# S5 layer: the late halves' entries moved ahead of all sixteen gate tiles, their copies split between ScalarE and VectorE

## The reference, cut to what matters

```python
pz = h @ w_in                     # D_MODEL -> 2 * E_WIDTH (E_WIDTH = 2048)
p, z = pz[..., :-E_WIDTH], pz[..., -E_WIDTH:]
# s5_mixer: u = p in 128 groups of 16 channels; for both directions:
def step(h, u_blk):
    bu = einsum('btgn,gpn->btgp', u_blk, bbar)      # enter the state space
    bu = bu.at[:, 0].add(abar[None] * h)
    _, hs = associative_scan(_linrec_combine, (a, bu), axis=1)   # recurrence
    y = einsum('btgp,gnp->btgn', hs, cmat).real      # leave it
...
g = gelu(y);  y = g * sigmoid(g @ w + bias)
x = layer_norm(alpha * x + gate * ((y * silu(z)) @ w_out), ...)
```

## Time and profile before

| | us |
|---|---|
| median of 3 runs | 2491.09 |
| lowest and highest | 2489.82, 2499.41 |
| profiled execution, its own time | 2490.22 |
| its span (first to last instruction) | 2488.4 |
| PE busy | 2179.3 (88%) |
| DVE busy | 1347.8 (54%) |
| ACT busy | 903.2 (36%) |

### The profile page before, as it was taken

The page is one execution under the profiler, slowest core; times in us unless marked ns, Lnnn a source line. Parts: engine busy times, 40 slices in busy tenths (PEclk is TensorE's granted clock), DMA queues, the critical chain, the costliest instruction groups (busy, mean ns, idle before and its releaser), DMA issues.

```text
span 2488.4 us, 33930 instructions
## 1 busy us (share of the span) xinstructions
PE 2179.3 (88%) x13589; PEld 1657.1 (67%) x13589; DVE 1347.8 (54%) x2633; ACT 903.2 (36%) x1779; POOL 445.0 (18%) x417
## 2 busy tenths in 40 slices
PE   6969897878989996899798976999999997878998
PEld 5847676647646695798453433678888864547998
DVE  4639676655578849454334456433333334455555
ACT  3325454542222273443222434222222212444443
POOL 0037969508911000000000000000000000000000
PEclk8989999989999998899899977899999998978999
DMA  8163545595687658865621312422323432224653
GB/s 276 57 204 108 168 122 143 163 275 180 213 268 219 193 197 320 232 170 181 192 68 51 102 35 87 131 93 86 96 81 93 115 102 85 85 81 140 196 162 118
DMA packets 434035, 366.34 MB, mean 147 GB/s; under 512 B 66238, under 2 KB 412622, under 8 KB 431702
## 3 DMA queue, kind: packets, MB, share of 16 engines
q1 hardware_dynamic: 392212, 320.87, 41.8%
q0 software_dynamic: 7424, 26.38, 2.9%
q10 hardware_dynamic: 34242, 16.92, 2.4%
HBM read 317.58 MB, written 54.92 MB: 150 GB/s over the span
## 4 chain that ended last, share of the span: by engine, by line
PE 68%; DVE 16%; ACT 6%; DMA 5%; POOL 2%; issue 2%; ACTq 1%; SPq 0%; DVEq 0%; POOLq 0%
PE ps L119 65%; DVE A L88 6%; PE ps L122 3%; ACT A L115 3%; POOL A L88 2%; DVE R L88 2%; DVE A L102 1%; DVE A L105 1%; DVE A L92 1%; DMA A<-btab 1%; DVE A L93 1%; DMA wbuf<-in_ada_w 1%; ACT A L116 1%; DVE A L96 1%; DMA xs<-X 1%
## 5 line engine op out<-in xcount | busy, mean ns | idle before, releaser
L119 PE MATMUL ps<-R,R 128*128 128x256 f32 (+1 forms) x3968 | 845.6, 335 | 35.5 <-ACT R L115 25.1
L119 PEld LDWEIGHTS ps<-R,R 128*128 128x128 f32 x3968 | 632.1, 193 | 109.6 <-ACT R L115 30.3
L119 PE MATMUL ps<-HR,R 128*128 128x512 f32 (+1 forms) x1984 | 556.8, 365 | 30.7 <-DVE R L88 20.5
L88 DVE TENSOR_TENSOR R<-wbuf,R 128x1024 fp32r<-128x1024 f32 (+2 forms) x304 | 349.5, 1158 | 350.6 <-ACT R L115 350.3
L119 PEld LDWEIGHTS ps<-HR,R 128*128 128x128 f32 x1984 | 358.1, 193 | 89.8 <-issue 23.8
L115 ACT ACTIVATE A<-ps 128x512 f32<-128x512 f32 (+4 forms) x400 | 210.2, 557 | 544.2 <-PE ps L119 400.0
L115 ACT ACTIVATE R<-wbuf 128x1024 fp32r<-128x1024 f32 (+2 forms) x304 | 270.1, 894 | 281.8 <-PE ps L119 255.6
L88 DVE TENSOR_TENSOR A<-A 128x128 f32<-128x128 f32 (+4 forms) x868 | 321.7, 402 | 87.9 <-ACT A L115 58.5
L119 PE MATMUL ps<-H,wbuf 128*128 128x512 f32 (+2 forms) x928 | 336.1, 519 | 13.5 <-DVE H L93 13.4
L119 PE MATMUL ps<-A 128*128 128x64 f32 (+11 forms) x1896 | 292.5, 355 | 27.2 <-DVE A L88 7.7
L88 POOL TENSOR_TENSOR A<-A 128x512 f32<-128x512 f32 (+3 forms) x186 | 218.0, 1184 | 522.2 <-DVE A L96 260.6
(11 more groups left out here) (114 smaller groups left out, 1630.6 us busy)
## 6 DMA issues: line engine op xcount, KB each, us to landing
wbuf<-in_w_ada SPq DMA_DIRECT2D x48, 1024.0 KB, 5.2
wbuf<-in_ada_w SPq DMA_DIRECT2D x24, 1024.0 KB, 8.8
wbuf<-in_w_out SPq DMA_DIRECT2D x24, 1024.0 KB, 5.6
wbuf<-in_w_ffn_gate SPq DMA_DIRECT2D x22, 1024.0 KB, 5.3
wbuf<-in_w_ffn_up SPq DMA_DIRECT2D x22, 1024.0 KB, 5.4
wbuf<-in_w_ffn_down SPq DMA_DIRECT2D x32, 704.0 KB, 4.7
wbuf<-in_attn_w_in SPq DMA_DIRECT2D x20, 1024.0 KB, 7.0
ctab<-A ACTq DMA_DIRECT2D x64, 256.0 KB, 2.8
```

Source lines behind the costliest of these rows:

```text
L88: return self.op(lambda e: e.tensor_tensor(out, a, b, op))
L119: return self.op(lambda e: e.matmul(out, lhsT, rhs, start=start, stop=stop, skip_group_check=True))
```

## The change

Three things change, all in the S5 class. The late units' entries stand in a row, with turns two units ahead and no gate tile between them. Units 16 to 21 are copied by ACT, units 22 to 31 by DVE (`BY_ACT`), behind `recur 0` on DVE. And all sixteen gate tiles stand behind the entries, on PE, ACT and SP. Nothing is computed in another way.

```diff
     def enter_pe(self, pe, u):
         q = u // 8
-        late = u >= 16
-        p = self.PS.take(pe, ("in", u), (self.act_evac if late else self.dve_evac, ("in", u)))
+        p = self.PS.take(pe, ("in", u), (self.act_evac if u in self.BY_ACT else self.dve_evac, ("in", u)))
...
+    BY_ACT = range(16, 22)
+
     def enter_dve(self, dve, u):
         if u == 0:
             dve.wait_mark("ln1")
-        if u < 16:
+        if u not in self.BY_ACT:
             self.enter_copies(dve, u, dve.copy, self.dve_evac)
 
     def enter_act(self, act, u):
         if u == 16:
             act.wait_ge(self.tr_done, ("bt", 15))
-        if u >= 16:
+        if u in self.BY_ACT:
             self.enter_copies(act, u, lambda d, s: act.act(d, s, ACT.Copy), self.act_evac)
...
-        dve.wait_ge(*((self.act_evac if hf else self.dve_evac), ("in", 16 * hf + 15)))
+        dve.wait_ge(self.dve_evac, ("in", 16 * hf + 15))
+        if hf:
+            dve.wait_ge(self.act_evac, ("in", self.BY_ACT[-1]))
...
-            if u < 16:
-                some(1 + (u // 2 + 1) % 2)
+            some(1 + (u // 2 + 1) % 2)
             for i in (u, u + 1):
-                if i + 4 < 16 or 20 <= i + 4 < 32:
+                if i + 4 < 16:
                     part("back", i + 4)
                 part("enter", i)
...
-        for i in range(8):
-            halves(u, lambda: step(z))
-            u += 2
+        part("turn", 16)
+        part("turn", 17)
+        for u in range(16, 32):
+            if u + 4 < 32:
+                part("back", u + 4)
+            if u + 2 < 32:
+                part("turn", u + 2)
+            part("enter", u)
         e.mark("in")
         part("recur", 1)
         part("before", 0)
         rest(z)
```

## The result

The changed kernel takes 2514.08 us (median of 6; 2509.75 to 2517.18), against 2491.78 for the kernel before in the same series: the ratio is 1.008, with a 95% interval of 1.0059 to 1.0100. That is slower by about 0.8%, where 2505.4 with a range up to 2511 was forecast. The profiled execution took 2515.54 us.

The account below looks back on a forecast made before the run. Two clocks were taken to bound the stage: the second recurrence and, hardly behind, panels issued after the last gate tile. Gate tiles 17.7 us later put the stage's end at +15.2: 2490.2 + 15.2 = 2505.4 us, own range 2500 to 2510.

Parts of the forecast that it names:

- What bounds the kernel: Stage from 855 to 1014 us: one clock from the second recurrence's start, one from the gate tiles' end, hardly behind.
- Step 1: Late units' entries: PE waits for DVE until 897.2, loses 1.8 us to the clock, ends entry 31 at 915.2.
- Rival C: PE stays at 0.50 from 897.2 through entry 31: 2520 us, or 2512 if only half; chance 0.09.
- Step 2: All 16 gate tiles behind entry 31 take 55.6 us and end at 970.8, 17.7 us later than before.
- Step 3: Leaves 0 and 1 take 26.7 us behind the gate tiles; leave 2 starts at 1004.0, 9.3 us later.
- Step 4: Leaves 2 and 3: last panel comes 54.6 us behind the last gate tile; end at 1029.3, +15.2 us.
- Step 5: Behind leave 3, from the GLU's first panel on: no slack, so the 15.2 us shift passes through whole.
- A: Last panels are not what leave 3 waits for; PE's pace sets the end: +6.8 us, 2497.0; chance 0.20.
- B: The second recurrence still ends the stage, so its 10 us come through: 2480.3 us; chance 0.06.
- D: Late unit loads leave PE no stop at turn 27: entry 31 at 913 to 916, same result within 2 us.

Follow-up runs that it names:

- j_warm18: Changed kernel with 18 repeats of turn 27's first four transposes, keeping PE at work in its stop: stage 202.0 us, ratio 1.0078 to the kernel before.
- a_again: The changed kernel run once more with no edit: stage 202.6 us, ratio 1.0095 to the kernel before.
- f_gates2: Changed kernel with two gate tiles put back ahead of turn 20: stage 195.8 us, ratio 1.0057 to the kernel before.
- i_before_again: The kernel before run once more with no edit, as its own comparison: stage 185.9 us, ratio 1.0003.
- c_halfrec: Changed kernel with the second recurrence cut to two of its four operations a step: stage 204.5 us, ratio 1.0090 to the kernel before.
- b_warm: Changed kernel with seven repeats of turn 27's first four transposes in PE's stop: stage 204.7 us, ratio 1.0076 to the kernel before.
- g_allact: Changed kernel's order with all late copies on ACT, none on DVE: stage 199.6 us, ratio 1.0065 to the kernel before.

## Why the prediction was right or wrong

**What bounds the kernel** (two clocks, the panels' hardly behind the recurrence's): right, and shown by the cut recurrence in both kernels and by the 57.5 to 62.4 us that follow the last gate tile in every profile with that panel order.

**Step 1, the entries: this is the step that failed, by the size of one term, the low clock behind the stop.** The release at 897.2 was right (906.15 less the 8.93 of offset is 897.2), the work behind it too (16.3 measured in j_warm18, 16.2 said). The clock was mis-sized. I took 3.6 us at half rate, from the stop ahead of leave 2, hence 1.8 us; it was 12.3 us at half rate, hence 6.1 (6.0 by j_warm18): 4.3 us more. In front of it, my "PE restarts after standing some 7 us" was 3.0 in the profile (6.7 in a_again, 8.6 in f_gates2), with the same low clock behind all of them. One other stop was the wrong sample: how long the clock stayed low was not the same from place to place. Rival C priced nearly this (half of the 16.2 us of work at 0.50, 2512; it was 6.1 of them), and I had given it 0.09, on the argument that PE works without gaps behind the release. It did, and the clock was low all the same. That the late load of unit 20 would cost nothing was right: the wait for DVE covered it. Entry 31 ended at 919.5 in the old count (829.68 + 89.83) instead of 915.2.

**Step 2, the gate tiles**: 55.3 against 55.6, right. They end 21.6 us later than before instead of 17.7; the difference is step 1's.

**Step 3, leaves 0 and 1**: 26.4 us behind the gate tiles against 26.7; leave 2 starts 32.9 behind them against 33.2: right.

**Step 4, leaves 2 and 3**: the last panel was used 54.3 us behind the last gate tile (1037.99 less 983.67) against 54.6: right. (PE's restart at 1035.33 is that for the panel before it. The clock was low there too, but PE reached the last panel just as it landed, so that cost the end little or nothing.) From there the end took 3.4 us instead of 3.9. Together 57.7 against 58.5. So the stage grew by 18.5 us, where 15.2 was said: 4.3 more by the clock, 1 less by the other terms.

**Step 5, behind it**: nothing there took part (1472.3 against 1474.4). But 18.5 us are 0.74%, and the medians say 22.3, in a_again 25.8. Both intervals of the changed kernel (1.0059 to 1.0100, 1.0072 to 1.0118) hold 0.74%; the second does not hold the 0.67% that the stage of i_before_again gives. Of the 8.7 us between 2505.4 and 2514.08, the stage has 3.3, 1.6 are the median of before in this series (2491.78 against 2490.2), and 3.8 are not in the two profiles' stages. By the stage alone the time would have been 2508.7, inside my range. The 3.8 I can't assign: the shared code ahead of the stage took 829 to 839 us with no kernel to it, and I had given a range for the stage alone, with nothing for that scatter. That is the second thing the forecast lacked.

**Rivals.** A (the leaves catch up): no, leave 3 waited 1.47 and 3.31 us for panels. B (the recurrence ends the stage): no, cutting it by 25 us left the stage at 204.5 (c_halfrec). C: came true for the clock, as said. D: the stop was there in every profile of that order, and its width changed nothing (3.0 to 8.6 us, entry 31 always at +89.7 to +89.9).

## What to carry to other kernels

When the chain of waits shows one engine bare at the end of a stage, look whether a second thing, here a full DMA queue with its own starting shot, ends within a few microseconds of it; cutting the bare engine's work in half shows at once how much it is worth. Work that is moved off a stretch must leave no gap there: the eight gate tiles hid the waits of their stretch, and with them gone PE lost 8.9 us idle and 12.7 us by its clock. When a loss lies ahead of a wait that would have come anyway, it costs nothing; look which wait ends last. Here the mark that starts many loads, the last gate tile, set the end of the stage, and the start of the second recurrence did not.

## What the runs showed of the hardware

How long PE ran at 1.2 GHz after a restart was not one number: 3.7 us of work behind 14.83 us idle, but 12.3 us behind 2.97 us idle and 13.2 behind 5.91 us in the changed kernel, with PE in work without a pause. Behind DVE's release it was 11.9 to 12.3 us in five profiles (after, a_again, b_warm, c_halfrec, f_gates2), behind stops of 2.97 to 8.61 us. Behind the wait for unit 20, 5.26 to 5.91 us long, it was 13.2 us in three (after, c_halfrec, j_warm18), 7.2 in a_again and 3.6 in two (b_warm, g_allact), with the same instructions. Nor did it take a long stop: in g_allact the granted clock fell to 0.50 behind waits of 1.04 and 0.85 us. The Trainium skill, in "TensorE: Matmul & The Clock Gate", section "What's actually happening", has activity release the throttle; the traces agree that it comes back, but PE was in work for 12 us, by its busy time, before it did.

From issue to landing the same panel of 1024 KB, number 23, took 8.4 us in the kernel before and 16.0 in the changed one, with DMA full in both.
